# The index mask in a three-operand form, and the head turns put around the pooling products

## The reference, cut to what matters

```python
# pooling: a windowed mean less the input, a 128x128 matrix per group, a scale per channel
mixed = ((cs - lag) / cnt - ug)
y_pool = concatenate([mixed_g @ pool_w[g] for g in range(4)]) * pool_scale
# index: for each row the 64 best of the admissible keys
rel = relu(einsum('bthd,bsd->bths', qi, ki))
score = where(adm, einsum('bths,bth->bts', rel, wi) * idx_scale, -inf)
_, sel = top_k(score, 64)
# attention over the selected keys only, 8 heads of 64
y_attn = softmax(q . k[sel] / 8) @ v[sel]
x = x + concatenate([y_pool, y_attn]) @ w_out
```

## Time and profile before

| | us |
|---|---|
| median of 3 runs | 754.18 (752.66 to 754.76) |
| the profiled execution, device time | 750.68 |
| its span in the trace | 748.9 |

### The profile page before, as it was taken

The page is one execution under the profiler, slowest core; times in us unless marked ns, Lnnn a source line. Parts: engine busy times, 40 slices in busy tenths (PEclk is TensorE's granted clock), DMA queues, the critical chain, the costliest instruction groups (busy, mean ns, idle before and its releaser), DMA issues.

```text
span 748.9 us, 12990 instructions
## 1 busy us (share of the span) xinstructions
PE 691.6 (92%) x5377; PEld 544.4 (73%) x5378; DVE 362.5 (48%) x719; ACT 325.2 (43%) x691; POOL 69.7 (9%) x76
## 2 busy tenths in 40 slices
PE   5889999999999999999999889997999999878786
PEld 3686677977999999999878767876865555535352
DVE  3458968756544555544589789334431111011011
ACT  2347536845444444333668886667321111101011
POOL 0400002020000002000200046261000000000000
PEclk9799999999999999999999999999999999989897
DMA  9997988529666745444664355559889999999996
GB/s 336 353 404 287 415 306 305 186 92 370 224 236 233 251 171 169 170 141 147 235 201 152 112 170 177 183 215 386 339 344 423 420 421 420 420 421 421 421 405 210
DMA packets 76706, 211.42 MB, mean 282 GB/s; under 512 B 7463, under 2 KB 34245, under 8 KB 62822
## 3 DMA queue, kind: packets, MB, share of 16 engines
q1 hardware_dynamic: 75602, 209.91, 74.6%
q0 software_dynamic: 800, 0.63, 0.5%
q10 hardware_dynamic: 244, 0.03, 0.0%
HBM read 209.51 MB, written 1.05 MB: 281 GB/s over the span
## 4 chain that ended last, share of the span: by engine, by line
PE 62%; DMA 14%; DVE 11%; ACT 5%; SPq 4%; issue 2%; POOL 1%; ACTq 0%; DVEq 0%; POOLq 0%
PE ps L1994 9%; PE ps L1995 9%; PE ps L1996 9%; PE ps L2730 5%; PE ps L2007 4%; PE ps L2008 4%; PE ps L2009 4%; SPq L460 4%; DMA ring<-in_expert_w_up_dram 4%; DMA ring<-in_expert_w_gate_dram 4%; DVE YT L1359 3%; DMA Z<-in_expert_w_up_dram 3%; DVE ring_low L1243 3%; PE ps L2772 2%; DMA ring<-in_w_in_dram 2%; PE ps L2695 2%
## 5 line engine op out<-in xcount | busy, mean ns | idle before, releaser
L1243 DVE TENSOR_TENSOR ring_low<-ring,HI 128x1024 fp32r<-128x1024 f32 (+1 forms) x119 | 142.6, 1240 | 22.8 <-ACT HI L727 22.8
L727 ACT ACTIVATE HI<-ring 128x1024 fp32r<-128x1024 f32 (+1 forms) x135 | 133.6, 1055 | 27.8 <-DMA ring<-in_w_in_dram 27.8
L1994 PE MATMUL ps<-AH,HI 128*128 128x256 f32 (+1 forms) x328 | 92.6, 282 | 0.5 <-DVE Z L1512 0.5
L1996 PE MATMUL ps<-AH,ring_low 128*128 128x256 f32 (+1 forms) x328 | 92.0, 280 | 0.0
L1995 PE MATMUL ps<-AL,HI 128*128 128x256 f32 (+1 forms) x328 | 91.8, 280 | 0.0
L2730 PE MATMUL ps<-ring,ZM 128*32 128x256 f32 x880 | 70.2, 412 | 12.8 <-DMA ring<-in_expert_w_up_dram 9.0
L1994 PE MATMUL ps<-HI,AH 128*128 128x512 f32 x160 | 66.1, 413 | 2.2 <-DVE ring_low L1243 1.0
L2007 PE MATMUL ps<-AH,HI 128*128 128x256 f32 x192 | 58.1, 303 | 7.8 <-DVE AL L1329 5.7
L1994 PEld LDWEIGHTS ps<-AH,HI 128*128 128x128 f32 (+1 forms) x328 | 61.3, 187 | 3.3 <-issue 2.5
L1995 PE MATMUL ps<-ring_low,AH 128*128 128x512 f32 x160 | 63.6, 398 | 0.0
L2730 PEld LDWEIGHTS ps<-ring,ZM 128*32 128x32 f32 x880 | 33.6, 118 | 38.9 <-DMA ring<-in_expert_w_up_dram 12.8
(11 more groups left out here) (398 smaller groups left out, 1262.8 us busy)
## 6 DMA issues: line engine op xcount, KB each, us to landing
ring<-in_expert_w_up_dram SPq DMA_DIRECT2D x28, 1024.0 KB, 22.0
ring<-in_expert_w_gate_dram SPq DMA_DIRECT2D x27, 1024.0 KB, 26.2
ring<-in_expert_w_down_dram SPq DMA_DIRECT2D x24, 1024.0 KB, 22.4
ring<-in_w_ffn_in_dram SPq DMA_DIRECT2D x20, 1024.0 KB, 5.9
ring<-in_w_in_dram SPq DMA_DIRECT2D x18, 1024.0 KB, 6.2
ring<-in_ada_w_dram SPq DMA_DIRECT2D x16, 1024.0 KB, 9.3
ring<-in_w_ffn_out_dram SPq DMA_DIRECT2D x11, 1024.0 KB, 7.3
ring<-in_ada_w_dram SPq DMA_DIRECT2D x16, 512.0 KB, 10.7
```

The source lines that it names most:

```text
L727: act(HI[:, (i + 1) % UNITS, 0:w], W.view(name)[:, o:o + w], ACT.Copy).then_inc(s_hi, 1)
L1243: tt(W.low(name)[:, o:o + w], W.view(name)[:, o:o + w], HI[:, (i + 1) % UNITS, 0:w].bitcast(F32), ALU.subtract).then_inc(s_lo, 1)
L1994: mm(dst, lh, rh, start=start, stop=False)
L1996: return mm(dst, ll, rh, start=False, stop=stop)
```

## The change

- `index_mask` no longer is a `tensor_scalar` with two constants but a `scalar_tensor_tensor`: compare the score with a constant, multiply by a second tensor. This one is a new third column of the small tile `eps`, which holds -1e30, read as if it were as wide as the scores. GpSimd sets it once, early.
- PE turns the queries' heads ahead of the `pm` products and the keys' heads between `pm` and `pw`.
- ACT copies QT, then MT, then KT, then AH (before: MT, QT, AH, KT).
- The two `low_out` no longer stand behind the seventh and the eighth round but behind the mask.
- GpSimd's semaphore numbers of `s_set` behind the new write go up by one.

```diff
-        eps = sb("eps", [P, 2])
+        eps = sb("eps", [P, 3])
...
+            po.wait_ge(s_set, BLK - 1)
+            po.memset(eps[:, 2:3], OTHER).then_inc(s_set, 1)
...
-            for h in range(2):
-                ac.wait_ge(s_plp, h + 1)
-                act(MT[:, 2 * h:2 * h + 2, :], ps[h][:, :].rearrange("p (g n) -> p g n", g=2), ACT.Copy).then_inc(s_pl, 1)
...
             heads_copied(QT, 0)
+            for h in range(2):
+                ac.wait_ge(s_plp, h + 1)
+                act(MT[:, 2 * h:2 * h + 2, :], ps[h][:, :].rearrange("p (g n) -> p g n", g=2), ACT.Copy).then_inc(s_pl, 1)
+            heads_copied(KT, 1)
             for kk in range(2):
                 ac.wait_ge(s_plp, 2 + kk + 1)
...
-            heads_copied(KT, 1)
...
-                    ts(SX[:, 1, t, 0:w], SX[:, 0, t, 0:w], -2.0e38, -1.0e30, ALU.is_gt, ALU.mult).then_inc(s_ix, 1)
+                    stt(SX[:, 1, t, 0:w], SX[:, 0, t, 0:w], -2.0e38, eps[:, 2:3].to_broadcast([P, w]), ALU.is_gt,
+                        ALU.mult).then_inc(s_ix, 1)
...
             for i in range(8):
                 index_round(i)
-                if i > 5:
-                    low_out(OP_POOL + i - 5, i - 6, i - 4, C2[:, PSC:PSC + 4])
...
+            ve.wait_ge(s_set, BLK)
             index_mask()
+            for i in range(2):
+                low_out(OP_POOL + i + 1, i, i + 2, C2[:, PSC:PSC + 4])
...
+            te.wait_ge(s_hq, 8)
             te.wait_ge(s_rel, 8)
+            turn_heads(512, (4, 5))
             te.wait_ge(s_z, 12)
             te.wait_ge(*W.ready("pm"))
...
-            te.wait_ge(s_hq, 8)
-            turn_heads(512, (4, 5))
+            te.wait_ge(s_hk, 8)
+            turn_heads(1024, (6, 7))
             te.wait_ge(*W.ready("pw"))
...
-            te.wait_ge(s_hk, 8)
-            turn_heads(1024, (6, 7))
```

More of the change, by code:

```diff
@@ L353, in build @@
         s_set = sem("s_set")
-        IDENT, MATS, PAD, MASKED, BLK, PAIRS_FF, PAIRS_F, GAINED, ROUTER = 2, 6, 7, 8, 11, 14, 17, 18, 23
+        IDENT, MATS, PAD, MASKED, BLK, PAIRS_FF, PAIRS_F, GAINED, ROUTER = 2, 6, 7, 8, 12, 15, 18, 19, 24
         s_hi, s_lo, s_lp, s_un, s_t0 = (sem(n) for n in ("s_hi", "s_lo", "s_lp", "s_un", "s_t0"))
@@ L655, in _ @@
             po.memset(blk, 0.0).then_inc(s_set, 1)
-            po.wait_ge(s_set, BLK - 2)
+            po.wait_ge(s_set, BLK - 3)
             po.memset(blk[0:64, :][:, 0:64], 1.0 / 64).then_inc(s_set, 1)
             po.memset(blk[64:128, :][:, 64:128], 1.0 / 64).then_inc(s_set, 1)
+            po.wait_ge(s_set, BLK - 1)
+            po.memset(eps[:, 2:3], OTHER).then_inc(s_set, 1)
             po.wait_ge(s_mxp, 2)
```

## The result

The changed kernel takes 757.22 us in the median of 20 runs (750.57 to 760.79), the kernel before 752.65 (748.88 to 756.69). The ratio is 1.0049 with a 95% interval of 1.0028 to 1.0069: 2 to 5 us slower, 3.7 in the middle. (The ratio isn't that of the medians, which lie 4.6 us apart.) The forecast was +1.9 on 754.18, that is 756.1, with a range of 751.5 to 757.8.

A forecast was written before the change was run, and what follows sets the result against it. The prediction took a chain through PE to bound the kernel up to about 550 us, then the experts' transfers. 2.06 us gained on PE and 4.0 lost to the mask's wait made 754.18 + 1.9 = 756.1 us, range 751.5 to 757.8.

The forecast's parts named there:

- What bounds the stretch: Up to about 550 us a chain through PE; shifts before 507 us move the experts' transfers and the end one for one.
- The turns and copies: On PE and ACT: the queries' turn fills a gap, PE no longer waits for KT; head scores 2.06 us earlier.
- The mask waits: On VectorE: each mask half waits for a GpSimd unit, 5.0 us the pair; PE starts the projection 1.9 us later.
- The row of `tensor_tensor`: VectorE's L1243, two SBUF inputs, taken as nearest price for the mask: 1.22 us, but 3.44 us beside GpSimd.
- The order at the boundary: GpSimd's unit begins 0.1 us before the mask arrives, and this repeats; rivals: VectorE first, chance 0.10, mask passed over, 0.08.
- The sum: 2.06 us gained on PE, 4.0 lost to the mask's wait: 1.9 us later at the projection and the end.
- The forecast's case: Mask waits one GpSimd unit per half, PE's projection start 1.9 us late; chance 0.65.
- "within 0.3%": Outcome for the whole kernel: time within 0.3%, 2.3 us, of the kernel before; chance 0.63.
- "slower": Outcome for the whole kernel: over 0.3%, 2.3 us, slower than before; chance 0.28, the passed-over case included.

The follow-up runs named there:

- second trace: The changed kernel with nothing altered, measured and profiled once more; 754.88 us, ratio 1.0036 against the kernel before.
- turns alone: Kernel before with only the moved turns and copies; tensor_scalar mask, low_out behind the seventh and eighth round as before; 753.39 us, ratio 0.9994.
- before with the pause: Kernel before, with GpSimd doing its attn0 and attn1 units only once the mask is written; 752.07 us, ratio 0.9987.
- lock probe: Changed kernel plus 16 GpSimd units in a row, each waiting for the one before, and 16 VectorE mask instructions of 256 columns; one run, 802.03 us.
- with the pause: Changed kernel, with GpSimd doing its attn0 and attn1 units only once the mask is written; 751.89 us, ratio 0.9955.
- old form: Changed kernel with the mask again a tensor_scalar with two constants, low_out still behind it; two sets: 752.82 us, ratio 0.9988, and 758.12 us, ratio 1.0059.
- gap filled: Changed kernel with 32 transposes of a constant on PE between head scores and projection; two sets: 757.95 us, ratio 1.0043, and 756.5 us, ratio 1.0034.
- AL ahead: Changed kernel with the two low_out between the eighth round and the mask, mask in its new form; 751.85 us, ratio 0.998.

## Why the prediction was right, and where it was short

The measured 757.22 us lies 1.1 us above the forecast's 756.1, and part of that closeness is luck. Two errors offset each other. The base, 754.18 us, was the median of three runs; over 20 runs the kernel before has 752.65, 1.5 us less. And the change cost 3.7 us where the sum has 1.9. On the base of 752.65 the same sum gives 754.6, 2.7 us short. The mechanism came out as described, up to PE's start on the projection; what follows goes through it.

- *What bounds the stretch, and that a shift before 507 us reaches the end one for one*: the shift at the experts' first transfer is the whole shift of PE. Behind it the span to the first output transfer (L603) is 272.2 us in before and 272.2 in the changed kernel's second trace, so nothing is given back. In its first it is 275.4, with two drops of the clock to half, near 522 and 553 us, that the second hasn't; two kernels whose PE isn't held ahead of the projection have such a pair too (turns alone 276.2, before with the pause 275.5). A further drop, near 423 us, is in five traces, whose GpSimd begins at 443.8 to 444.5 us rather than at 439.9 to 442.4. Traces with one such drop, near 542 to 553 us, have 273.2 to 273.8 us there (five of them), those with none 272.1 to 273.2 (five), those with two 275.4 to 276.2 (four, the lock probe among them). I take these for chance; together they would make up most of the 8 us over which one kernel's times spread, but that wasn't tested.
- *The turns and copies, 2.06 us*: right; 1.98 at the head scores in every trace with the moved turns, and -2.00 to -2.05 with the pause. That alone they are worth less, 0.7 to 0.9, was not in the prediction. A row was named for more than it shows: the earlier trace rows give "issue" for PE's 0.82 us of idle time; that the copy of u was late stands in ScalarE's timeline, where it ends at 449.30, 0.1 us before PE's start.
- *The mask waits, 5.0 us, PE's start +1.9*: right in both traces, 4.89 and 4.88 us and +2.07 (+1.92 by PE's product). Laid on before's clock by that product, the mask came at 454.8 and PE started the projection at 460.6, as forecast. Two slips on the way did no harm: L1243's unit ended 1.13 us after GpSimd's next was begun, not 1.08; and 453.71 plus 1.26 us is 454.97, not 454.89. The row of `tensor_tensor` was the right neighbour: a spread column is a second SBUF input like any other. The Trainium skill, page "SBUF — State Buffer", section "Who interferes with whom", says that a VectorE instruction with two SBUF inputs contends with a GpSimd one that reads SBUF. The traces agree for the spread column: 0.32 us for the mask's first half while GpSimd paused, 1.9 to 7.0 us in every trace in which a unit was at work when it came.
- *The order at the boundary*: here the chances were wrong. I reasoned that both clocks start from the same event, so the order should repeat, and that a waiting instruction gets in at the first chance. But the start isn't fixed: in the changed kernel's two traces GpSimd's first unit waits for one of VectorE's units of low parts (3.3 us), in those of the old form and the first with the gap filled, for two (4.5 us); over all 14 traces it is one in seven and two in seven. The same event thus starts the clocks in two ways, 2.2 us apart for VectorE. The mask got in first (old form, both traces), waited a unit for each half (changed kernel, second trace with the gap filled), or was passed over once (turns alone, old form), twice (AL ahead, lock probe) or by all that GpSimd had left (first trace with the gap filled). With AL behind the mask these give -2.0, +2.1 and +4.8 us at the projection. The forecast's case is the middle one; the heaps in the times fit such a mixture, but that is an argument from few traces.
- *The sum*: this is where it fell short. It took idle time on PE to cost itself and no more. Its second price, 1.5 us at half clock behind the gap, was a term that the sum lacked: 2.07 + 1.55 = 3.6 us, against the ratio's 3.7. It takes the kernel from "within 0.3%" (0.63 in the forecast) to "slower" (0.28). The prediction had put nothing for the clock, and gave no reason for that. That this term is what moved the median isn't shown, since the filled kernels' medians are no lower.

## What to carry to other kernels

A three-operand form over SBUF doesn't get around GpSimd: what helps is to let GpSimd pause for the one instruction that others wait for, or to keep small results that PE needs ahead of an instruction that can be held. Work moved forward on one engine pays only if what comes next from the others is early too; look for the next two waits. When a change opens an idle stretch on PE, cost the stretch and then the clock that may be lower behind it. And count a shift from an event on the engine that carries it: counted from another engine's, it was off by up to 0.2 us here.

## What the runs showed of the hardware

- A VectorE instruction held off by GpSimd isn't next in line: with GpSimd's units back to back it waited through up to four of them (9.5 us for 0.3 us of work), in the old form (4.25 us) as in the new; where each unit waited for a semaphore of the one before, it got in at every boundary, 16 of 16.
- It goes the other way too: GpSimd's first unit waited for one of VectorE's units in half of the traces (3.2 to 3.3 us) and for a second one too in the others (4.3 to 4.5 us, for 2.4 us of work).
- TensorE's clock fell to its lower level for 3.4 us behind an idle stretch of 3.8 us in both traces of the changed kernel, and not where 32 transposes took that stretch, although in one of these 3.1 us of idle time remained behind them. It fell 0.6 and 0.9 us after PE was at work again. Behind an idle time of 1.8 to 1.9 us near 421 us it fell in five traces of 14.
